# An RWKV-7 mixer on one core: another order of its first and steady units, a program of its own for the last one

## What is computed

```python
def wkv_step(state, inp):
    r, w, k, v, a, b = inp
    sa = jnp.einsum('bhij,bhj->bhi', state, a)
    state = state * w[:, :, None, :] + sa[..., None] * b[:, :, None, :] + v[..., None] * k[:, :, None, :]
    return state, jnp.einsum('bhij,bhj->bhi', state, r)
...
    state, y = lax.scan(wkv_step, wkv0.astype(f32),
                        (tm(rh), tm(wh), tm(kh), tm(vh), tm(-kk), tm(kk * ah)))
    ...
    y = ((y - mean) * lax.rsqrt(var + LNX_EPS)).reshape(b, l, d) * lnx_w.astype(f32) + lnx_b.astype(f32)
    ...
    out = (y * g.astype(f32)).astype(h.dtype) @ w_o
```

## Time and profile before

| | us |
|---|---|
| runs | 2980.95, 2986.54, 2989.56 |
| median | 2986.54 |
| the profiled execution | 2989.93 |
| its span on the core | 2987.8 |
| mixer, first iteration, from the first product of unit 0 to the start of iteration (2, 1) | 2197.24 to 2251.57 |
| seven iterations (f = 2 to 8) | 2251.57 to 2490.66 |
| last iteration, to the barrier | 2490.66 to 2532.15 |

### The profile page before, as it was taken

How to read it: one execution, slowest core, us unless ns; L and a number is a source line. 1 busy time by engine, 2 the same in 40 slices (tenths; PEclk the granted TensorE clock), 3 DMA queues, 4 the chain that set the end, 5 groups by cost and what they waited for, 6 DMA issues and landing times.

```text
span 2987.8 us, 65947 instructions
## 1 busy us (share of the span) xinstructions
PE 2871.8 (96%) x27215; PEld 2751.3 (92%) x27215; DVE 2102.9 (70%) x2722; ACT 1349.0 (45%) x2409; POOL 696.1 (23%) x534
## 2 busy tenths in 40 slices
PE   8999999989999999999999999999988997999999
PEld 8999998679999998999999999999987776999999
DVE  6977866656666664697786878875456776487975
ACT  4434434455555552443444434442456673333432
POOL 1321310310000001132131213343034562211320
PEclk9999999999999999999999999999999998999999
DMA  3223222011111111122322222221200001223222
GB/s 121 96 89 99 88 73 80 23 52 30 43 36 37 43 58 57 57 96 89 99 88 82 86 85 95 89 86 70 107 2 19 19 19 56 78 78 100 88 87 83
DMA packets 78971, 208.10 MB, mean 70 GB/s; under 512 B 25505, under 2 KB 42274, under 8 KB 63714
## 3 DMA queue, kind: packets, MB, share of 16 engines
q1 hardware_dynamic: 78690, 204.16, 20.8%
HBM read 198.63 MB, written 5.49 MB: 68 GB/s over the span
## 4 chain that ended last, share of the span: by engine, by line
PE 86%; DVE 7%; ACT 4%; issue 3%; POOL 0%; DMA 0%; POOLq 0%; ACTq 0%; DVEq 0%; SPq 0%
PE PS L469 26%; PE PS L285 23%; PE PS L1595 12%; PE PS L2206 5%; PE PS L642 5%; PE PS L2535 4%; PE PS L1622 1%; PE PS L1574 1%; PE PS L2541 1%; PE PS L2186 1%; DVE DOWN L771 1%; DVE WL L269 1%; DVE WL L435 1%; ACT WH L264 1%; PE PS L1233 1%
## 5 line engine op out<-in xcount | busy, mean ns | idle before, releaser
L408 POOL TENSOR_TENSOR WLF<-RAW 128x512 f32<-128x512 f32 x72 | 94.1, 1307 | 982.7 <-PE PS L285 657.3
L264 ACT ACTIVATE WH<-RAW 128x1536 fp32r<-128x1536 f32 (+3 forms) x112 | 171.4, 1530 | 325.4 <-PE PS L285 196.0
L269 DVE TENSOR_TENSOR WL<-RAW,WH 128x1536 fp32r<-128x1536 f32 (+3 forms) x113 | 217.8, 1928 | 121.0 <-ACT WH L264 121.0
L1595 PE MATMUL PS<-UKMH,CTH 128*128 128x384 f32 (+1 forms) x768 | 269.0, 350 | 0.9 <-POOL RQL L1536 0.9
L469 PE MATMUL PS<-XH,WH 128*128 128x288 f32 x864 | 255.6, 296 | 8.3 <-DVE M L510 8.3
L1671 DVE TENSOR_REDUCE SS<-SQ 128x4 f32<-128x512 f32 x256 | 173.5, 685 | 120.5 <-ACT SQ L1654 118.8
L469 PE MATMUL PS<-XH,WL 128*128 128x288 f32 x864 | 256.0, 296 | 0.0
L469 PE MATMUL PS<-XL,WH 128*128 128x288 f32 x864 | 255.4, 296 | 0.0
L1595 PE MATMUL PS<-UKMH,CTL 128*128 128x384 f32 (+1 forms) x768 | 252.6, 329 | 0.0
L1654 ACT ACTIVATE SQ<-PS 128x384 f32<-128x384 f32 (+1 forms) x384 | 172.3, 455 | 130.3 <-PE PS L1595 130.0
L285 PE MATMUL PS<-HH,WH 128*128 128x288 f32 x1056 | 225.3, 294 | 1.1 <-DVE WL L269 1.1
(11 more groups left out here) (666 smaller groups left out, 8968.5 us busy)
## 6 DMA issues: line engine op xcount, KB each, us to landing
RAW<-in_w SPq DMA_DIRECT2D x113, 1024.0 KB, 4.8
RAW<-in_w SPq DMA_DIRECT2D x48, 768.0 KB, 5.0
ROWS<-in_cache_c SPq DMA_DIRECT2D x128, 128.0 KB, 2.0
RAW<-in_w SPq DMA_DIRECT2D x16, 512.0 KB, 4.6
KRS<-in_cache_kr SPq DMA_DIRECT2D x128, 32.0 KB, 1.8
RAW<-in_w SPq DMA_DIRECT2D x8, 384.0 KB, 3.3
X<-in_x SPq DMA_DIRECT2D x4, 576.0 KB, 7.6
out_y<-X SPq DMA_DIRECT2D x8, 288.0 KB, 2.3
```

The costliest lines, as they stand in the source:

```text
L264: act.activation(WH[n % 2][:, 0:cols], RAW[n % 2][:, 0:cols], ACT.Copy).then_inc(rounded, 1)
L269: dve.tensor_tensor(WL[n % 2][:, 0:cols], RAW[n % 2][:, 0:cols], WH[n % 2][:, 0:cols].bitcast(F32), ALU.subtract).then_inc(item_split, 1)
L1595: mm = pe.matmul(out[:, 0:c1 - c0], c[u][:, x], w, start=t == 0, stop=t == 5)
```

## The change

Units 2 to 8: NT and NR are made across (in the other head's rows), so RV and XA x RA change their rows too. The output y is summed in bank 4, the bank of the states, not 7. STC x QQ stands beside RV, vtok x mk1 beside NR x NT, R0 x mb1 beside NT x NR, XA x RA beside the next two products, and KTOKP x vtok beside N4R x PP. `gates` goes to bank 5 and moves from before z to behind X2. Unit 0: DVE splits the weights only after POOL's BT, splits TH and G1 later, and makes the sums and the direction of unit 1 earlier; rates(1) moves. The last unit has lists of its own. SP issues the first load of the output weights earlier. The core of the diff ("..." where lines are left out):

```diff
+    SQT_, OFF = blk("SQT_", 24), blk("OFF", 24)
+    N4RS = blk("N4R", 24), blk("N4R_LAST", 18)
...
+        dve.wait_ge(q["bt"], 1)
         dve.tensor_tensor(WL[1], LW2[:], WH[1][:].bitcast(F32), ALU.subtract).then_inc(lw_lo, 1)
+
+    def lora_in_lo_dve(dve):
         dve.tensor_tensor(THL[:], TH[:], THH[:].bitcast(F32), ALU.subtract).then_inc(th_split, 1)
...
+                sp.wait_ge(q["x"], x_of(KD, 4))
+                sp.dma_start(RAW[I_RO % 2][:], a["w"][row_of(I_RO), :, :]).then_inc(raw_in[I_RO % 2], 16)
...
+                    mm = pe.matmul(bank(5 if u else 2)[:, out], w[:, 1, p, :], x[:, cols], start=n == 0, stop=n == 2)
...
+        def crossed(c):
+
+            for r, out in zip(HEADS, HEADS[::-1]):
+                mm = pe.matmul(RA_PS[out, c], XA[r, c, :], RA[r, c], start=True, stop=True)
+            return mm
...
+
+            for r in HEADS:
+                mm = pe.matmul(cells(4)[r, c, :], STC[r, c - 1, :], QQ[r, c, :], start=c == 1, stop=False, skip_group_check=True)
...
-                        mm = pe.matmul(RA_PS[out, c], PP[r, c, :], RA[r, c], start=True, stop=True)
+                    for r in HEADS:
+                        mm = pe.matmul(RA_PS[r, c], PP[r, c, :], RA[r, c], start=True, stop=True)
...
-                pe.wait_ge(th_split, 2)
-                pe.wait_ge(lw_lo, 1)
                 keys(1)
-                wait("tac", 1)
-                rates(1)
                 wait("kk", kk_at(2, "max"))
...
+                pe.wait_ge(th_split, 2)
+                pe.wait_ge(lw_lo, 1)
+                wait("tac", 1)
+                rates(1)
...
-            if front:
-                gates(f)
-            state(7)
+            if front and not f:
+                gates(0)
...
-            for c in range(NB):
-                if prompt:
-                    x = products(1, at(OFF), at(XA), (c,))
-                if chain:
-                    sums(7, at(vtok_b), at(mk1), c, start=True)
-            if prompt:
...
+            if prompt:
+                wait("xa", xa_of(f, 2))
+                products(1, at(OFF), at(XA), across=True).then_inc(q["z"], 1)
+            state(7)
+            if prompt:
+                products(0, at(XA), at(OFF), across=True).then_inc(q["z"], 1)
...
-                for c in range(1, NB):
-                    mm = sums(7, lambda r, c: STC[r, c - 1, :], at(QQ), c, start=False, across=False)
+            for c in range(NB):
+                if front:
+                    x = products(6, at(MK0), at(vtok), (c,), across=prompt)
+                if chain and c:
+                    mm = queried(c)
+            if front:
...
+            if chain:
+                wait("y", 2 * b - 1)
             for c in range(NB):
                 if prompt:
                     x = products(0, at(NR), at(NT), (c,))
-                if front:
-                    mm = products(6, at(MK0), at(vtok), (c,), across=prompt)
-            if front:
-                mm.then_inc(q["rv"], 1)
+                if chain:
+                    sums(4, at(vtok_b), at(mk1), c, start=False)
...
+                if chain:
+                    mm = sums(4, at(R0), at(mb1), c, start=False)
...
-                wait("gg", n)
+                gates(f)
                 wait("pp", f)
                 wait("zc", 3 * f - 1)
-                products(2, at(N2R), at(PP)).then_inc(q["x"], 1)
+                wait("rvc", n)
+                for c in range(NB):
+                    x = products(2, at(N2R), at(PP), (c,))
+                    if c % 2:
+                        crossed(c // 2)
+                x.then_inc(q["x"], 1)
                 wait("xt", 2 * f)
-                products(0, at(N2T), at(N2R)).then_inc(q["x"], 1)
+                for c in range(NB):
+                    x = products(0, at(N2T), at(N2R), (c,))
+                    if c % 2:
+                        mm = crossed((NB + c) // 2)
+                x.then_inc(q["x"], 1)
+                mm.then_inc(q["ra"], 1)
...
-                wait("rvc", n)
+                wait("zc", 3 * f)
+                wait("xa", xa_of(f, 3))
                 if chain:
                     wait("y1c", b)
                 for c in range(NB):
-                    for r in HEADS:
-                        mm = pe.matmul(RA_PS[r, c], XA[r, c, :], RA[r, c], start=True, stop=True)
+                    x = products(2, at(N4RS[f // KD]), at(PP), (c,))
                     sums(4, at(KTOKP), at(vtok), c, start=True)
-                mm.then_inc(q["ra"], 1)
-                wait("zc", 3 * f)
-                wait("xa", xa_of(f, 3))
-                products(2, at(N4R), at(PP)).then_inc(q["x"], 1)
+                x.then_inc(q["x"], 1)
...
+        def final(b):
+            p = b - 1
...
+            wait("y_norm", y_at(b, "sq_lo"))
+            head_sums(5, YHZ, YLZ).then_inc(q["y_norm"], 1)
+            for x in range(2, len(RO_EARLY)):
+                out_part_mm(pe, x)
...
+                wait("y", 2 * b)
+                act.activation(flat(YH), bank(4), ACT.Copy).then_inc(q["y_norm"], 1)
+            if prompt:
+                gate(f)
...
+            if prompt:
+                wait("x", x_of(f, 4))
+                act.activation(flat(N4RS[f // KD]), bank(0), ACT.Copy).then_inc(q["zc"], 1)
+                wait("ra", f)
+                act.activation(RA[:], RA_PS, ACT.Copy).then_inc(q["rac"], 1)
             if chain:
                 wait("y_norm", y_at(b, "dev"))
-                act.activation(flat(yh), flat(Y1S[b % 2]), ACT.Square)
+                act.activation(flat(YH), flat(Y1S[b % 2]), ACT.Square)
                 act.activation(flat(Y3), flat(Y1S[b % 2]), ACT.Square).then_inc(q["y_norm"], 1)
...
+                lora_in_lo_dve(dve)
+                inverse_root(1, range(0, 2))
...
                     inverse_root(1, range(2, 4))
                     wait("ar1", 1)
                     running_sums(1)
+                wait("i4", n)
+                plus(XA, 0, "xa", xa_of(f, 2))
...
+            split_item(dve, I_RO)
+            inverse_part(p, 0)
+            wait("sf", b)
+            dve.tensor_tensor(flat(S0), flat(S0), bank(5), ALU.add).then_inc(q["sfa"], 1)
...
+            out_part_dve(dve, 5)
+            for k in range(4):
+                inverse_part(b, k)
+            scaled(b)
+            shifted(b)
...
+                if f == 1:
+                    wait("mk1", 1)
...
+            wait("sample_norm", 9)
+            pool.tensor_tensor(unit(RT, 0), unit(RT, 0), YS3[:], ALU.mult).then_inc(q["sample_norm"], 1)
+            wait("sample_norm", 10)
+            wait("final", 3)
+            pool.tensor_tensor(unit(RT, 0), unit(RT, 0), unit(KT, 0), ALU.mult).then_inc(q["sample_norm"], 1)
+            wait("sample_norm", 11)
+            pool.tensor_tensor(unit(RT, 0), unit(RT, 0), unit(VT_, 0), ALU.add).then_inc(q["sample_norm"], 1)
+            gate(b)
```

381 lines of the change are left out of this document (235 added, 146 removed).

## The result

Over eight runs of each kernel the median went from 2985.90 us to 2995.61 us; the ratio is 1.0029 with a 95% interval of 1.0020 to 1.0039. The range of 2968 to 2997 held it, the forecast of 2983 had the wrong sign. The profiled execution of the changed kernel took 2999.96 us (span 2998.0), 4.4 us above its own median and the slowest of its eight; so sums made from this trace come out a few us too large against the medians. Single executions that were slow from end to end at a lower clock (7281 us in e2, 4108 us in e7) don't enter the ratios.

The account below looks back on a forecast made before the run. PE and ACT were taken as full from X2 to md, PE as bound from md to X2. Terms +10.7 + 1.2 - 4.2 - 9.0 - 7.3 + 5.2 = -3.4 gave 2986.5, as a median 2983 us; range 2968 to 2997.

Parts of the forecast that it names:

- first units: Units 0 and 1: DVE's WL waits, so POOL's BT ends earlier and unit 1 starts earlier; -9.0 us, bounds -10.5 and -5.
- X2 to md: Seven stretches of the steady iterations: ACT's longer list delays squares, POOL's YL, DVE's scan and PP; +10.7 us.
- md to X2: Seven stretches of the steady iterations: PE's list loses the gates, stops for issue stay; -0.6 us a unit, -4.2 in all.
- unit 8's tail: Unit 8 to the last unit's start: same chain without table and sigmoids, 7.8 instead of 6.6 us; +1.2.
- last unit: Rounding and split run under the state chain, then DVE's list sets the end; -7.3 us, bounds -3 and -9.
- clock: PE's new 2.4 us wait before head_sums lowers the clock in half of seven units, 1.5 us each; +5.2 us.
- Pairing: Units 2 to 8: pairing products saves PE 2 phases, 1.9 us an iteration, all behind X2.
- (b): Steady iterations: as forecast, but the clock holds; 2978 us, or 2973 with a tail at its lower bound; chance 0.24.
- (c): Wait before second head_sums: clock falls in all seven units, scan slips more; 2993 us, or 2997; chance 0.18.
- (a): X2 to md: pairing pays in full, squares never waited for, -0.9 us a unit; 2961 us; chance 0.12.
- (d): Last unit doesn't get shorter, through ACT waiting for weights or DVE's list; -3 instead of -7.3, 2987 us; chance 0.06.

Follow-up runs that it names:

- e2: Changed kernel plus three matmuls on constants, result unused, on PE before the second head_sums wait of each of seven iterations; 2987.94 us, ratio 1.0004 to the kernel before.
- e7: Changed kernel with the second head_sums (variance) on PE moved behind the next iteration's product PP x RA; 2995.84 us, ratio 1.0027 to the kernel before.
- e3: Changed kernel with ACT's copy of RA moved behind the two squares instead of ahead of them; 2996.25 us, ratio 1.0028 to the kernel before.
- e5: Changed kernel with POOL's gating product moved behind XA of the next iteration; 2996.61 us, ratio 1.0025 to the kernel before.
- e10: Changed kernel with three unused matmuls before the second head_sums, POOL's gating product behind XA, DVE's last addition to PP ahead of the scan; 2984.74 us, ratio 0.9992.
- e8: Changed kernel, across pairing kept, with the iteration's tail reordered on ACT, PE, POOL and DVE; 2988.01 us, ratio 0.9995 to the kernel before.
- e1: Kernel before with only unit 0's new order and the last unit's own lists, units 1 to 8 as they were; 2976.85 us, ratio 0.9964.
- e14: e1 with ACT's table load and root of the variance moved behind the copy of VTOK; 2990.64 us, ratio 1.0012 to the kernel before.
- e17: Changed kernel, pairing kept, with a second reordering of the tail and ACT's root between the copies of STC and VTOK; 2981.58 us, ratio 0.9974.
- e16: e1 with ACT's table load and root of the variance moved between the copies of STC and VTOK; 2981.99 us, ratio 0.9976 to the kernel before.

## Why the prediction was wrong, by its own steps

The terms against the traces, as differences from before; the second column is the changed kernel, the third e2. The first units are taken up to X2 of unit 1, since its tail belongs to the next row; that is why they show 6.6 here and 8.3 at the start of iteration (2, 1):

| term | forecast | changed kernel | with the filler |
|---|---|---|---|
| first units, up to X2 of unit 1 | -9.0 | -6.6 | -8.0 |
| X2 to md, seven stretches | +10.7 | +23.8, the clock in it | +13.7 |
| md to X2, seven stretches | -4.2 | -2.4 | -5.7 |
| unit 8's tail | +1.2 | +2.4, the clock in it | +1.5 |
| last unit and the item behind it | -7.3 | -6.4 | -6.2 |
| clock | +5.2 | | 0 |
| sum | -3.4 | +10.8 | -4.7 |
| by the spans | | +10.2 | -5.4 |

**First units: right in the mechanism, the gain behind it too large.** WL waits, BT takes 1.27 us, and unit 1 starts at 2219.5 for 2218.8. No clock of 0.50 stands behind that, as said, which other traces of the same order don't all repeat; from md to X2 of unit 1 the gain was 0.8 us (19.05 for 19.80), where 1.6 and 1.0 were added.

**X2 to md: right in its chain, and nearly in its size at full clock.** The squares end at X2 + 6.4 (6.7 was said), POOL's YL is late, PE waits 1.8 us (2.4), DVE's scan and PP slip, and unit 2, the one without a lowered clock, took 14.83 us (14.6). With the clock held, e2 needs 3.0 us more than the term in seven stretches (+13.7): the scan took 1.8 us beside POOL's YL, where the 1.23 of the earlier trace rows was put in. What the step left out is ACT's own list up to UTS, which ends at the same point as the chain that it followed. "From there to md nothing changes" held for PE, and BT was later than the 14.6 said (14.9 in the shown unit, 15.4 in e2). ACT's share is why the single repairs (e3, e5, e7) and the pair of them (e10) did little or nothing. ACT's list alone would have given about the same 15: in the unit of the earlier trace rows it reached UTS just ahead of md, at X2 + 13.8, and two copies of 0.6 us come on top. Two slips of size stand beside this. Pairing was put at 1.9 us of PE's time a unit; at full clock e2's seven iterations have PE busy for 222.29 us, 10.9 of them with the filler, so 211.4 for 217.39, which is 0.9 a unit. And rival (b)'s 2973 should read 2971 by its own terms (2978 less 10.7, plus 4).

**The clock: the term that failed.** By the traces it is the largest of the misses, and one of size: the place and the mechanism were right. It had the fall in half of seven units, at 1.5 us each, +5.2 in all. It fell behind the second head_sums of units 3 to 8, and for 6.83 us at a time in five of these, where the forecast knew 3.3 and 3.4 from the earlier trace rows. At half speed 6.83 us hold 3.4 of work, more than twice the 1.5. By the ratios the clock costs 7.5 us (e2); by the two traces it is 10.1 between X2 and md alone, 8.5 of them in the six stretches with a filler in e2. Rival (c) had this place, this mechanism and this sign; it priced a fall by 3.4 us as well, came to 2993, or 2997 with the first units at their bound, and stands nearest to what was measured. It deserved more than 0.18: its own condition, a wait of about 2 us, was met by the 2.4 us that the forecast itself reckoned. As a border that condition isn't borne out: the clock fell behind waits of 1.33 and 1.77 us, and five waits of 1.6 us in e8 had no fall behind them.

**md to X2.** -5.7 at full clock (142.3 us for 148.0), -2.4 in the changed kernel, -4.2 forecast; both lie in the bounds of 0 and -7. The reason given holds: in the seven iterations PE's stops for issue over 0.2 us sum to 16.8 us before and 17.0 after, while its waits for a result went from 0.8 to 17.4, 12.8 of these for POOL. The traces show what these stops go with. All 26 of before ended 2.2 to 3.0 us behind the start of a 16 KB instruction fetch (DMA queue 8); the 0.82 us of the earlier trace rows ended 2.6 us behind that of 2373.70. By the rule that the prediction took from the Trainium skill ("Runtime: NRT & Kernel Launch", Instruction fetch mechanics), fetches mostly hidden, the term would have been -7; the changed kernel and e2 didn't come to that.

**Last unit: right in the mechanism.** DVE's list sets the end, but its four reciprocals begin 30.8 us behind the unit's start (27.5 was said) and in e1, where no lowered clock runs into the unit, 29.0.

**The sum.** In terms of the traces the forecast missed by 14 us: 2.4 in the first units, 7.9 in X2 to md with the clock, 1.2 in unit 8, 1.8 in md to X2, 0.9 at the end. All five went one way, so the clock alone doesn't carry the miss: of the 7.9, 3.0 are the chain at full clock and 4.9 the clock. With the clock held (e2) the other terms of the forecast sum to -8.6 and stand beside -4.7 in the trace, and e2's ratio is 1.0004, not below 1: e2's profiled execution was 3.6 us below its median and that of before 4.0 above the median of its eight, and these two make up the difference. So e2 supports the terms as sizes in a trace, to some 4 us and no better. By the ratios the miss splits in another way: the two ends bring -10.8 us (e1) for the forecast's -16.3, the clock costs 7.5 (e2) for 5.2, and the steady units at full clock take what is left, some 12 for 7.7 (+10.7 + 1.2 - 4.2). Each of these carries an interval of 3 to 5 us. That the ends, the tail and the clock all came out on the slow side of the forecast is shown by both; how much each of them missed is not.

**The rivals.** (a) fell: ACT was the bound, as the argument against it said. (b) is what e2 makes by force, and it came out at 2988 instead of 2978. (c) held, in six units of its seven; that its 2993 to 2997 hit the 2995.6 so closely is in part luck, since it took the first units and the last one over from the forecast. (d) fell: 6.4 of the 7.3 us came.

## What to carry to other kernels

When an edit saves time on an engine that is busy throughout, add up the other engines' lists over the same stretch first: ACT was busy for 83.47 of 90.89 us, and two copies of 0.6 us more in it gave back what the matmul phases less had saved on PE. A wait of 1.3 to 2.7 us that an edit puts into TensorE's list is to be priced with a lowered clock behind it, 1.7 to 3.4 us, in most iterations: six of seven in the changed kernel, five of six in e14. It can stay away (e8), so the price is a bound. Where three chains end within 0.5 us of each other, moving one shows nothing; only the row that names the last releaser after each repair tells which is next. A step that must move belongs into a gap that the trace shows (1.68 us here), and what overwrites its input says how late it may go.

## What the runs showed of the hardware

- Three matmuls an iteration whose result nobody reads made the kernel 7.5 us faster; in their trace the granted clock was 1.00 (2.4 GHz) over all seven iterations, against 0.92.
- The granted clock stood at 0.50 for 3.41, 6.83, 10.24 or (before, last unit) 13.65 us at a time. Behind idles of 0.79 and 1.77 us (changed kernel) and 1.33 (e3) it fell; behind 1.76 in unit 2 of the changed kernel, 1.57 and 1.59 in e2, and five of 1.6 in e8 it didn't. The length of the last idle alone doesn't tell.
- In seven iterations TensorE stopped for issue for 15 to 17 us, paired or not (stops over 0.2 us). In the kernel before each of the 26 stops ended 2.2 to 3.0 us behind the start of a 16 KB instruction fetch.
- From one execution of the changed kernel to another the time ranged over 8.4 us (2991.55 to 2999.96), with mean clocks from 0.983 to 0.987, and the slowest had 0.983.
- DVE's scan takes 1.22 us alone and 2.19 beside a product on POOL, and three DVE subtractions of 1.18 us take 3.98 beside three products on POOL.
- With straight and across products paired (e17 against e16, which differ in the order of the tail too) PE's busy time in seven iterations was 8.4 us less, and its idle time 13.6 more.
